# Down-projection of a two-layer decoder trunk: the residual's multiply-add on VectorE, a third step prepared earlier, two lower quarters summed by VectorE instructions, and the output rows stored step by step

## What is computed

```python
up = jnp.einsum('btd,df->btf', x, w_up)
hp = jnp.concatenate([conv_prefix, up], axis=1)
hc = conv_b + sum(conv_w[i] * hp[:, i:i + T] for i in range(CONV_WIDTH))
new_conv = hp[:, -(CONV_WIDTH - 1):]
g, u = hc[..., :D_FF], hc[..., D_FF:]
y = jnp.einsum('btf,fd->btd', jax.nn.gelu(g, approximate=False) * u, w_down)
x = layer_norm(DEEPNORM_ALPHA * x + y, ln2_g, ln2_b)
```

## Time and profile before

| | us |
|---|---|
| median of 3 runs (lowest, highest) | 2284.81 (2284.01, 2285.26) |
| the profiled execution | 2284.06 |
| its span | 2282.3 |
| mean granted TensorE clock, share of full speed | 0.98 |
| TensorE busy in the span | 2153.5 (94%) |
| VectorE busy | 1606.6 (70%) |
| ScalarE busy | 1044.2 (46%) |
| GpSimd busy | 860.4 (38%) |

### The profile page before, as it was taken

The page is one execution under the profiler, slowest core; times in us unless marked ns, Lnnn a source line. Parts: engine busy times, 40 slices in busy tenths (PEclk is TensorE's granted clock), DMA queues, the critical chain, the costliest instruction groups (busy, mean ns, idle before and its releaser), DMA issues.

```text
span 2282.3 us, 35355 instructions
## 1 busy us (share of the span) xinstructions
PE 2153.5 (94%) x13884; PEld 1939.1 (85%) x13884; DVE 1606.6 (70%) x2084; ACT 1044.2 (46%) x1863; POOL 860.4 (38%) x538
## 2 busy tenths in 40 slices
PE   7999999899999999899989999989999999989996
PEld 7997677899999998688788867779999999967785
DVE  1477767877777777676636687577778777775675
ACT  3226655544344444345522276464444443444552
POOL 1115255554554551321121252546445545430301
PEclk9999999999999999999999999999999999999998
DMA  5303066245555558987861212643455455598967
GB/s 158 86 25 86 26 205 178 66 111 140 143 125 131 141 128 286 253 213 185 198 163 48 56 42 95 175 148 85 118 141 143 116 145 145 137 290 248 221 156 188
DMA packets 255005, 327.92 MB, mean 144 GB/s; under 512 B 39920, under 2 KB 158448, under 8 KB 254768
## 3 DMA queue, kind: packets, MB, share of 16 engines
q1 hardware_dynamic: 223288, 261.70, 36.4%
q0 software_dynamic: 31552, 63.97, 17.4%
HBM read 217.65 MB, written 98.03 MB: 138 GB/s over the span
## 4 chain that ended last, share of the span: by engine, by line
PE 69%; DVE 15%; ACT 6%; DMA 4%; issue 3%; POOL 2%; SPq 2%; ACTq 0%; DVEq 0%; POOLq 0%
PE ps L2677 35%; PE ps L2769 11%; PE ps L2357 10%; PE ps L2616 4%; DVE al L1959 1%; PE ps L2420 1%; PE ps L2500 1%; DVE dl L1955 1%; PE ps L2526 1%; SPq L734 1%; DMA araw<-a_scr 1%; PE ps L2793 1%; DMA rz_top<-gain 1%; PE ps L2515 1%; DVE mrow L1645 1%
## 5 line engine op out<-in xcount | busy, mean ns | idle before, releaser
L2677 PE MATMUL ps<-bt,bh 128*128 128x272 f32 (+1 forms) x3520 | 593.5, 290 | 15.9 <-DVE bt L1864 7.6
L2677 PEld LDWEIGHTS ps<-bt,bh 128*128 128x128 f32 x3520 | 505.3, 190 | 17.6 <-DVE bt L1864 8.0
L1277 ACT ACTIVATE bh<-wblk 128x512 fp32r<-128x512 f32 x308 | 183.2, 623 | 490.7 <-POOL wblk L983 290.8
L2677 PE MATMUL ps<-bt,bl 128*128 128x272 f32 (+1 forms) x1760 | 370.2, 290 | 0.0
L2769 PE MATMUL ps<-dh,ah 128*128 128x512 f32 x616 | 248.7, 404 | 37.1 <-DVE al L1959 26.7
L2677 PEld LDWEIGHTS ps<-bt,bl 128*128 128x128 f32 x1760 | 279.7, 191 | 0.0
L971 POOL TENSOR_TENSOR bl<-wblk,bh 128x512 fp32r<-128x512 f32 x98 | 160.7, 1642 | 294.7 <-ACT bh L1277 294.7
L1882 DVE TENSOR_TENSOR bl<-wblk,bh 128x512 fp32r<-128x512 f32 x210 | 162.1, 805 | 140.0 <-ACT bh L1277 140.0
L2769 PE MATMUL ps<-dl,ah 128*128 128x512 f32 x616 | 245.3, 398 | 0.0
L2769 PE MATMUL ps<-dh,al 128*128 128x512 f32 x616 | 245.3, 398 | 0.0
L2677 PE MATMUL ps<-ba,bh 128*128 128x272 f32 (+2 forms) x1408 | 236.2, 290 | 4.1 <-DVE gu L1905 2.4
(11 more groups left out here) (268 smaller groups left out, 4295.3 us busy)
## 6 DMA issues: line engine op xcount, KB each, us to landing
wblk<-in_w_up SPq DMA_DIRECT2D x88, 512.0 KB, 6.0
a_scr<-hg SPq DMA_DIRECT2D x44, 552.0 KB, 3.7
e_scr<-hg POOLq DMA_DIRECT2D x44, 512.0 KB, 5.9
araw<-a_scr SPq DMA_DIRECT2D x66, 256.0 KB, 4.6
w<-in_w_down SPq DMA_DIRECT2D x66, 256.0 KB, 5.1
araw<-e_scr SPq DMA_DIRECT2D x66, 256.0 KB, 4.1
w<-in_w_down POOLq DMA_DIRECT2D x16, 1024.0 KB, 9.9
wrow<-in_w_out SPq DMA_DIRECT2D x48, 256.0 KB, 5.2
```

Of the source, the lines that this page charges most:

```text
L1277: act.activation(bh[b][:], block_of(f, b), ACT.Copy).then_inc(S["u_hi"], 1)
L2677: e = nc.tensor.matmul(up_half(f, b, n), lhs, rhs[:, c:HW_] if n else rhs[:, 0:c], start=(k == 0 and m == 0), stop=(k == HK - 1 and m == 2))
```

## The change

- **Residual.** The multiply moves from GpSimd to VectorE as `scalar_tensor_tensor` with ALPHA folded in: in step 9 for tile 8 (two instructions), in steps 13 to 16 for tiles 0 to 3, in 29 to 31 for tiles 4 to 6 and in 36 for tile 7. `scaled_gains` on ACT goes; ALPHA is folded into `first_out` and `row_lo` as well, which become `scalar_tensor_tensor`. The loads of x (`z_back`) of tiles 0 to 3 move on SP from steps 6 to 9 to steps 9 to 12, `first_join` from steps 16 to 19 to steps 17 to 20. `R_P1T` now waits for the residual that VectorE does in step 16.
- **Third step.** ACT and DVE prepare the steps 0, 1 and 2 during the last up-projection slice; `gelu(21)` moves to step 1, behind `dh` and `ah` of step 3; `sample_hi`/`sample_lo` 1 move to step 3 and the negation behind them to step 4.
- **Sum of products.** `R_U3B` and `R_U3C` go. `sum_join` adds `un` on VectorE: two tiles of the one half in step 67, two in 69; two of the other half in 74 and two in 75.
- **Stores.** `y_rows` of the TOP tiles is issued on SP behind `act_block` of the steps 66, 68, 70, 72 and 74, no longer behind all of them and the first weights of the next layer (`pair_in`).

```diff
 # SP
-                    elif 6 <= s < 10:
-                        z_back(l, s - 6)
+                    elif 9 <= s < 13:
+                        z_back(l, s - 9)
...
+                    if 66 <= s < 76 and s % 2 == 0:
+                        y_rows(l, TOP[(s - 66) // 2])
...
-                for t in TOP + [5] + BY_DVE:
+                for t in [5] + BY_DVE:
                     y_rows(l, t)
 # POOL
                 act_add(l, KP - 2, 1)
-                residual(l, NB)
                 act_add(l, KP - 2, 2)
                 act_add(l, KP - 1, 0)
-                residual(l, 0)
                 act_add(l, KP - 1, 1)
-                residual(l, 1)
                 weight_add(l, T_1, 0)
-                residual(l, 2)
                 act_add(l, KP - 1, 2)
-                residual(l, 3)
                 weight_add(l, T_1, 1)
                 residual_add(l, R_P1T)
...
-                residual_add(l, R_U3B)
-                residual_add(l, R_U3C)
 # ACT
-                        for s in range(2):
+                        for s in range(3):
                             down_hi(l, s)
                             act_hi(l, s)
...
-                    if s + 2 < NST:
+                    if 3 <= s + 2 < NST:
                         down_hi(l, s + 2)
                         act_hi(l, s + 2)
-                    if s == 0:
+                    if s == 1:
                         gelu(l, FT - 1)
 # DVE
+            def residual(l, t):
+
+                rz, q = rzd[t][0:tokens(t), :], tokens(t)
+                dve.wait_ge(S["gain_landed"], 64 * l + 32)
+                dve.wait_ge(S[zb_of(t)], zb_count(l, t))
+                dve.scalar_tensor_tensor(out=rz, in0=rz, scalar=ALPHA, in1=gain[0][0:q, :], op0=ALU.mult, op1=ALU.mult).then_inc(S["xp"], 1)
+                if t == NB:
+                    dve.wait_ge(S["xp"], xp_n(l, NB))
+                    dve.scalar_tensor_tensor(out=rz, in0=gain[1][0:q, :], scalar=ALPHA, in1=rz, op0=ALU.mult, op1=ALU.add).then_inc(S["xp"], 1)
...
+            def sum_join(l, i, half):
+
+                dve.wait_ge(S["joins"], JOINS * l + J_U3 + i + 1)
+                dve.wait_ge(S["xp"], xp_n(l, 4 + i) + 1)
+                rz = half_of(4 + i, half)
+                dve.tensor_tensor(rz, rz, un[:, i, :], ALU.add).then_inc(S["joins"], 1)
...
                     elif s == 8:
                         sample_lo(l, 3)
+                    elif s == 9:
+                        residual(l, NB)
...
+                    elif 13 <= s < 17:
+                        residual(l, s - 13)
+                    elif 17 <= s < 21:
+                        first_join(l, s - 17)
...
+                    elif s in (67, 69, 74, 75):
+                        for i in range(2):
+                            sum_join(l, (67, 69, 74, 75).index(s) % 2 * 2 + i, s < 70)
```

More of the change, by code:

```diff
@@ L75 @@
 RESID = [8, 0, 1, 2, 3, 4, 5, 6, 7]
-R_P1T, R_U3B, R_U3C, RADDS = 1, 2, 3, 3
+R_P1T, RADDS = 1, 1
 P1_EV = 6
@@ L1008, in act_add @@
                     pool.dma_start(f_scr[k], e_scr[k, :, 2, :], accum_op=ALU.add).then_inc(S["adds2"], 16)
-            def residual(l, t):
-                rz, q = rzd[t][0:tokens(t), :], tokens(t)
-                if t == NB:
-                    pool.wait_ge(S["gain_ok"], 4 * l + 2)
-                pool.wait_ge(S[zb_of(t)], zb_count(l, t))
-                pool.tensor_tensor(rz, rz, gain[0][0:q, :], ALU.mult).then_inc(S["xp"], 1)
-                if t == NB:
-                    pool.wait_ge(S["xp"], xp_n(l, NB))
-                    pool.tensor_tensor(rz, rz, gain[1][0:q, :], ALU.add).then_inc(S["xp"], 1)
             def residual_add(l, which):
@@ L1024, in residual_add @@
                 after(pool, "radd", 16 * (n - 1))
-                if which == R_P1T:
-                    pool.wait_ge(S["p1_ev"], P1_EV * l + 4)
-                    pool.wait_ge(S["xp"], xp_n(l, 3) + 1)
-                    out, src = rz_top[:, :, HT:D], p1[:]
-                else:
-                    pool.wait_ge(S["joins"], JOINS * l + J_U3 + 4)
-                    out, src = rz_bot[:, :, HT:D] if which == R_U3B else rz_bot[:, :, 0:HT], un
+                pool.wait_ge(S["p1_ev"], P1_EV * l + 4)
+                pool.wait_ge(S["xp"], xp_n(l, 3) + 1)
+                out, src = rz_top[:, :, HT:D], p1[:]
                 pool.dma_start(out, src, accum_op=ALU.add).then_inc(S["radd"], 16)
@@ L1171, in x_hi @@
                 act.wait_ge(S["x_tr"], x_n(l, t) + 1)
-                if l and t in (0, 4):
-                    act.wait_ge(S["radd"], 16 * (RADDS * (l - 1) + (R_U3C if t else R_P1T)))
+                if l and t == 0:
+                    act.wait_ge(S["radd"], 16 * RADDS * l)
                 src = x_bank(l, t).rearrange("p b (k t) -> p b k t", t=P)[:, :, :, 0:tokens(t)]
@@ L1705, in row_lo @@
             def row_lo(l):
-                dve.wait_ge(S["gain_ok"], 4 * (l + 1))
-                dve.tensor_tensor(dbl[:], gain[1][:, HT:D], dbh[:].bitcast(F32), ALU.subtract).then_inc(S["p1_ev"], 1)
+                dve.wait_ge(S["gain_ok"], 2 * (l + 1))
+                dve.scalar_tensor_tensor(out=dbl[:], in0=gain[1][:, HT:D], scalar=ALPHA, in1=dbh[:].bitcast(F32), op0=ALU.mult, op1=ALU.subtract)\
+                    .then_inc(S["p1_ev"], 1)
             def first_join(l, i):
@@ L2240, in body @@
                     if last:
-                        down_lo(l, 1)
-                        act_lo(l, 1)
+                        for s in range(1, 3):
+                            down_lo(l, s)
+                            act_lo(l, s)
                     if f:
@@ L2288, in body @@
                         stats(l, TOP[s - 24], 0)
+                    elif 29 <= s < 32:
+                        residual(l, s - 25)
                     elif s == 32:
                         sample_part(l, 2, 1, P_SAMP[P_3])
+                    elif s == 36:
+                        residual(l, 7)
                     elif s in (33, 34):
```

38 lines of the change are left out of this document (14 added, 24 removed).

## The result

| | before | changed |
|---|---|---|
| median of 4 runs each (lowest, highest), us | 2284.41 (2282.83, 2285.26) | 2261.12 (2256.45, 2265.12) |
| ratio, 95% interval | | 0.9898 [0.9877, 0.9919] |
| the profiled execution, us | 2284.06 | 2262.6 |
| its span, us | 2282.3 | 2260.9 |

The change makes the kernel 1.0% faster, 23 us where 51.8 were forecast.

What follows compares the result with a forecast made beforehand. TensorE, busy 94% of the span, was taken as the bound, with its waits and low clock to win: 10.0 + 15.0 + 18.1 + 2.7 + 7.05 − 1.0 = 51.8 us, so 2233 us, range 2222 to 2250.

Steps and rivals of the forecast that it cites:

- What it frees in steps 4 to 43: Residual moved to VectorE, both down-projections: removes TensorE's waits and low clock there, 15.0 and 18.1 us won after tile 8's price.
- The price of tile 8's residual: Step 9, ahead of the sample's join in step 10: its 2.5 us make that join about 0.6 us late.
- The first steps: First four steps of each down-projection: 19.2 us becomes 14.2, so 5.0 us a layer, 10.0 in all.
- the two small waits at steps 3 and 4: Late `al(3)` and `al(4)` at the start of each down-projection: 1.5 us allowed for both, from 0 to 4.
- The hold of VectorE: Steps 9 to 36: GpSimd's residual lengthens `al` and `dl`; without it none over 1.3 us. Rival of another cause: 2256, 0.06.
- The small stores: SP's 18 stores in step 18: 8 us or less instead of 12.58 and 14.47, as `R_P1T` starts later.
- the rival on them: Small stores stay slow and step 19's block lands late: 8.7 to 11.3 us given back, 2243; chance 0.15.
- End of layer 0: Last joins after `sum_join`: 2.7 us won if GpSimd's two `wl` hold VectorE, 5.7 with no hold.
- End of layer 1: Last steps: 7.05 us won by the sum, less a 1.0 us wait from the stores in steps.
- the chain holds SP: Layer 1's `gained` chain lands 5 us later, steps 75 and 76 wait 4.6 us: 6 us more, 2239; chance 0.18.
- The low clock that the rival had: Steps 75 and 76 of layer 1, behind their 4.6 us wait: TensorE at the low clock for 2.6 us.
- The forecast of 7.05 us for the sum itself: End of layer 1, sum of products on VectorE: last joins start at 2255.0 instead of 2262.05.

Runs made afterwards that it cites:

- r7: Changed kernel with the residual of tile 8 on VectorE in step 7 instead of step 9: 2251.74 us, ratio to before 0.9848.
- r7_late_y: Changed kernel with tile 8's residual in step 7 and the TOP tiles' stores behind all act_blocks again: 2244.47 us, ratio to before 0.9824.
- x12: Kernel r7_late_y with the loads of x in steps 12 to 15 and residuals 0 to 3 in steps 14 to 17: 2240.53 us, 0.9806.
- late_x: Kernel r7_late_y with the loads of x in steps 13 to 16 and residuals 0 to 3 in steps 17 to 20: 2246.89 us, 0.9833.
- zb: Changed kernel with the four loads of x back in steps 6 to 9: 2261.95 us, ratio to before 0.9886.
- only_T: Kernel before with the early third step alone: 2284.78 us, ratio to before 0.999.
- no_T: Changed kernel without the early third step: 2268.12 us, ratio to before 0.992.
- only_R: Kernel before with the residual on VectorE alone, and its loads of x in steps 9 to 12: 2268.19 us, ratio to before 0.9924.
- only_S: Kernel before with the sum of products on VectorE alone: 2269.77 us, ratio to before 0.9934.
- late_y: Changed kernel with the stores of the TOP tiles behind all act_blocks again: 2251.61 us, ratio to before 0.9846.

## Why the prediction was wrong

**What failed is one sentence: "What it frees in steps 4 to 43 is the whole 15.6 and 18.7 us, if the rest stays hidden."** I had named what hides VectorE's new work, but not asked what TensorE would meet next once VectorE was no longer late. It was a small load behind full DMA engines, and behind it VectorE's own new instructions. Of the 33.1 us of this term 14.5 came, so 18.6 of the 22.6 us are missing in it. The runs say where: moving tile 8's residual out of step 9 gives 9.7 of them back (`r7`), moving the loads of x behind the small load 5.7 more (`r7_late_y` to `x12`), and `x12` is still 5.9 above the forecast in the two layers together (133.8 and 132.9 us where 130.4 each were forecast), 4.6 of it in steps 12 to 18.

The DMA share stood in the rows that I quoted, 0.95 and 0.93 at the start of layer 0, and it should have made me ask. It doesn't decide by itself. TensorE has stretches with such a share and not one wait, steps 4 to 8 of the changed kernel and steps 9 to 11 of `x12`:

```profile
897.46:913.73 16.27, 16.27 (x72) 13.41 (x73) 10.05 (x17) 6.36 (x12) 2.42 (x2) 1.00 1.05 353
910.50:920.04 9.54, 9.54 (x44) 7.87 (x42) 6.61 (x11) 3.66 (x7) 2.19 (x2) 1.00 1.05 321
```

What decided was which bytes stand ahead of the transfer that is waited for: `late_x` and `x12` put 1.5 MB behind the small load instead of ahead of it and get 4.2 to 4.7 us for it at step 11; `zb` leaves them ahead and gets nothing.

**The price of tile 8's residual was off by a factor of eight.** I put it at 0.6 us a layer; `r7` shows 4.8 and 5.2. Behind the late load it stood just between the last `al` and the join that TensorE waits for, so in layer 1 its 2.4 us counted in full (4.0 to 1.6) and in layer 0 half (2.8 to 1.6), and the low clock behind the waits came on top: after 2.78 and 2.82 us TensorE ran at 1.2 GHz for a stretch, after the 2.00 and 1.60 of `r7` at 2.4. What tile 8's residual would cost in step 9 with the load in time no run shows.

**The first steps: right,** 8.4 of 10.0 us, with the two small waits at steps 3 and 4 (0.48 and 0.40 us) where I had put them. But what they win is not all kept: alone 6.0 of 10.8 us are left at the end of the two down-projections, and the median is lower by no more than the noise (`only_T`); in the changed kernel 6.8 of 9.6 are left (`no_T`). I had added the terms as if they were independent. That the early step alone meets the same hold was to be read from the order: the hold begins with the gains (step 6), not with TensorE.

**The hold of VectorE: right.** That GpSimd's residual holds VectorE is shown by three kernels: with it 7.36 us (`only_T`), without it 686 ns on the mean (`only_R`, changed). One thing is left over: between GpSimd's two instructions lie 1.30 us with a DMA issue in them, in `only_T` and before, and the held `al`, 0.68 us long by itself, did not end in them; no run says why. The small stores came out nearly as forecast (8 us or less): 7.13 us in layer 0 and 8.50 in layer 1 instead of 12.58 and 14.47, and no wait at step 19; the rival on them has fallen.

**End of layer 0: right in size by luck,** 2.2 of 2.7 us. The hold by `wl` happened, as the earlier trace rows had it: one `sum_join` took 2.89 us, over GpSimd's first `wl` of 2.52. By the rule of the Trainium skill (SBUF — State Buffer, section "SBUF: two separate sides") a VectorE instruction with two SBUF inputs and a GpSimd instruction that reads SBUF exclude each other; the trace agrees, 2.89 us for the held `sum_join` and 0.68 for the join with one input in `ps`. In the forecast I let both `wl` go first; in fact three `sum_join` had started before the first. So the joins lost less than forecast, and TensorE's 3.7 us for `wl` are gone besides. The mean granted clock of the crossing, 0.88 where it was 0.95 before, hid the difference: at 1.00 (`only_S`, `r7_late_y`) the crossing takes 26.8 us, 4.9 less than before. What I had not seen is that the stores land earlier by themselves once `un` is gone (`only_S`, `late_y`), so that the stores in steps bring nothing there.

**End of layer 1: the rival "the chain holds SP" came true in part.** I allowed 2 us of delay for the chain's last landing and 1.0 of wait. The links took 6.6 us instead of 5.2, and the waits were 1.64 and 0.72; with what follows them, `late_y` puts the price of the stores at 3.3 us. The low clock that the rival had did not come. The forecast of 7.05 us for the sum itself was met by `only_S` (7.4).

**The rest** was 7.7 us longer in the profiled execution. Four profiles of the fourteen (`zb`, with all of the change, and that of before among them) took 16.7 us for the matmuls 1101 to 1200 of the program, in the attention part of layer 0, the other ten 20.6 to 22.5. In the changed kernel VectorE was held there:

```profile
192.70 3.11 DVE L2078 TENSOR_TENSOR Sb<-Sb,ast 128x1024 f32<-128x1024 f32 x1
```

while GpSimd ran

```profile
190.30 2.14 POOL L969 TENSOR_TENSOR qr<-qr,swq 128x512 f32<-128x512 f32 x1
192.40 2.34 POOL L943 TENSOR_TENSOR wl<-wraw,wh 128x1024 fp32r<-128x1024 f32 x1
```

The instructions are the same in all kernels. I read the difference as one of order: which of the two comes first there is a matter of fractions of a microsecond. No run varies that order alone. Whether the changed kernel meets the longer case more often than that of before, whose runs reached from 2278.7 to 2292.5 us on the other chips, stays open: there is one profile of it. 3 us more of the 7.7 are a stretch at the low clock at 1184 to 1190 us (granted 0.50), behind small matmuls and with no wait ahead of it.

**A version that beats both** is `x12`: residual and sum on VectorE, third step early, tile 8 in step 7, loads of x in steps 12 to 15, stores where they were. 2240.5 us, 1.9% below before and 0.9% below the changed kernel.
